# A routed expert layer with 96 places per expert, and its product's bf16 cast on ScalarE

## The chip, the cores and the metric

The kernel runs on one core of a Trainium2 chip. The metric is the device time of one execution in microseconds (us), the median over runs. TensorE is called PE here, VectorE DVE, ScalarE ACT, GpSimd POOL, SyncE SP.

## What is computed

The reference is two blocks of two layers each (two mixers of attention, two hybrid mixers of gated linear attention and a state space scan), each layer with a feed-forward network. The last of the four feed-forward networks is a mixture of eight experts, and the change lies there alone:

```python
def swiglu_2(t, w_gate, w_up, w_down):
    return (jax.nn.silu(t @ w_gate) * (t @ w_up)) @ w_down

def moe_swiglu(h, router_w, w_gate, w_up, w_down):
    ...
    logits = (t @ router_w).astype(jnp.float32)
    top_v, top_i = lax.top_k(logits, TOP_K)
    top_p = jax.nn.softmax(top_v, axis=-1)
    gates = jnp.sum(jax.nn.one_hot(top_i, N_EXPERTS, dtype=jnp.float32) * top_p[..., None], axis=1)
    ...
    for e in range(N_EXPERTS):
        out = out + gates[:, e:e + 1] * swiglu_2(t, w_gate[e], w_up[e], w_down[e])
```

There are 256 tokens of 1024 values, a hidden width of 3584, eight experts and two experts per token. So 512 token copies are spread over the experts, 64 on average. With the reference's inputs the fullest expert gets 92. All weights and activations are float32.

## The kernel before, in words

**Splitting.** A float32 operand is taken as a sum of two bf16 numbers: hi is the value rounded to bf16, lo is the remainder. A product is made of three bf16 matmuls, hi by hi, hi by lo and lo by hi. For every weight, ACT makes hi (a cast) and DVE makes lo (the weight less hi).

**Places.** Router, counts and picks come first. Each expert has 128 places; the tokens that chose it are gathered by matmuls with 0/1 matrices into `he_hi` and `he_lo` (expert, k tile, place). The largest count is put in `COUNT`. If it fits into the places, `gathered` runs (from `moe_parts`, lines 1168 to 1375), else `general`, which sends all 256 tokens through every expert. PE, ACT and DVE each test this for themselves (lines 2388, 2397, 2408).

**Pieces.** An expert's hidden width is cut into 28 pieces of 128, 224 in all. A piece has 128 x 3072 float32 weights: gate and up (2048 columns, the front, 1 MB) and down (1024 columns, the back, 0.5 MB). SP loads them into a ring of four slots, `RING`, front and back by DMAs of their own, in the order front, back of the piece before, front (lines 341 to 350). A front slot comes free with DVE's lo (semaphore `front_used`), a back slot with DVE's lo of down (`back_used`).

**A pair of pieces** is the unit of all engines:

- PE, `up` (lines 1186 to 1197): 2 x 8 x 3 matmuls a piece; the weights stand still (128 x 128) and an expert's places stream (128 columns) into half of a bank of PSUM. PE then does `down` (lines 1199 to 1209) of the pair before: 6 matmuls a piece, the hidden values stand still (128 x 128 places) and 512 columns of down weights stream. So the order is up, up, down, down.
- ACT, `silus`: SiLU of the pair (line 1275, 256 columns for two pieces), then hi of gate/up of piece 4 (1264), hi of down of piece 2 (1270), gate/up 5, down 3 (counted from the pair's group of four).
- DVE, `gating`: `gate_pair` multiplies SiLU by up (1322), waits for its own result, casts it to bf16 (1325), makes its lo (1327); then come the four lo: gate/up 4 (1310), down 2 (1315), gate/up 5, down 3.

```python
dve.tensor_tensor(f, silu[p], hid(2 * i, 1, T), ALU.mult).then_inc(S.prod.sem, 1)
dve.wait_ge(S.prod.sem, m + S.prod.at(3))
dve.wait_ge(S.down_done.sem, 2 * m + S.down_done.at(0))
dve.tensor_copy(hi, f).then_inc(S.act_hi.sem, 1)
```

**Border of two experts.** DVE copies the expert's output out of PSUM (`keep_output`, 1331) after the first pair of the next one, and PE scatters it back to the tokens with 8 float32 products of 256 columns (`scatter`, 1214) before the next `down`. Seven borders lie inside the stage.

In the rows below the names are tiles: `weights` is the ring, `normed_or_mix` and `turned` hold the bf16 gate/up weights of slots 0, 1 and 2, 3, `aux` the bf16 down weights, `projected` the gathered tokens, `probs` the SiLU and the bf16 product, `probs_turned` the float32 product, `ps` is PSUM, `extra` the expert's output. The operation that the profile calls CAST or COPY on DVE is `tensor_copy`.

## Time and profile before

| | before |
|---|---|
| median of 3 runs | 2783.81 us (2783.21 to 2789.51) |
| span of the profiled execution | 2779.1 us (its own device time is not given apart) |
| PE busy | 2581.3 us, 93% of the span |
| PE weight loads | 1969.1 us, 71% |
| DVE busy | 1941.8 us, 70% |
| ACT busy | 1431.9 us, 52% |
| DMA | 674.36 MB, mean 243 GB/s |

The span runs from the first to the last instruction of one execution; the median comes from executions without a profiler and has some us around the span in it. Busy shares are averages over many stages with different limits. Matmuls are pipelined and their ends are modelled, so two matmuls of which each is shown 0.22 us long may start 0.06 us apart: PE's pace is read from starts.

### The profile page before, as it was taken

How to read it: one execution, taken by the hardware profiler on the slowest of the kernel's cores; microseconds unless marked ns; L12 is line 12 of the kernel's file. 1: busy time of each engine (PE TensorE's matmuls, PEld its weight loads, DVE VectorE, ACT ScalarE, POOL GpSimd, SP SyncE). 2: the span in 40 equal slices, each digit the busy share in tenths (PEclk: the TensorE clock that was granted, in tenths of full speed). 3: DMA queues.
4: the chain of work that ended last, by engine and by line, in shares of the span. 5: the costliest groups of instructions: out<-in, count | busy, mean ns of one | idle time of the engine just before them, and what ended most of it. 6: DMA issues, size and time to landing. Idle time of an engine off the chain costs nothing. (4 is left out here: it accounts for less than half of the span.)

```text
span 2779.1 us, 57909 instructions
## 1 busy us (share of the span) xinstructions
PE 2581.3 (93%) x22787; PEld 1969.1 (71%) x22998; DVE 1941.8 (70%) x2633; ACT 1431.9 (52%) x1753; POOL 14.9 (1%) x12
## 2 busy tenths in 40 slices
PE   6988899999887789998899999899999999999997
PEld 4646677676754467767677767678888888888886
DVE  3366555655535755555565555689999999999997
ACT  3245444443312554444354444377777676777774
POOL 0000000000200000000000000000000000000000
PEclk8979999999978999999899998889999999999999
DMA  7331555554366056544465544449999999999994
GB/s 290 143 161 35 216 199 201 209 201 173 109 229 271 1 201 222 194 162 181 164 251 199 192 168 182 152 178 404 386 395 383 375 392 376 392 381 379 393 376 192
DMA packets 121211, 674.36 MB, mean 243 GB/s; under 512 B 13488, under 2 KB 13968, under 8 KB 67088
## 3 DMA queue, kind: packets, MB, share of 16 engines
q1 hardware_dynamic: 120032, 664.47, 63.4%
q10 hardware_dynamic: 1072, 8.42, 0.8%
q8 instruction: 72, 1.18, 0.2%
q14 instruction: 35, 0.29, 0.0%
HBM read 671.79 MB, written 1.05 MB: 242 GB/s over the span
## 5 line engine op out<-in xcount | busy, mean ns | idle before, releaser
L940 PE MATMUL ps<-projected,normed_or_mix 128*128 128x256 bf16 x1504 | 409.9, 273 | 1.2 <-issue 1.2
L941 PE MATMUL ps<-projected,normed_or_mix 128*128 128x256 bf16 x1504 | 409.9, 273 | 0.0
L1194 PE MATMUL ps<-projected,normed_or_mix 128*128 (+1 forms) x1792 | 304.6, 220 | 3.3 <-DVEq L1342 3.3
L1196 PE MATMUL ps<-projected,normed_or_mix 128*128 (+1 forms) x1792 | 304.7, 220 | 0.0
L1195 PE MATMUL ps<-projected,normed_or_mix 128*128 (+1 forms) x1792 | 304.6, 220 | 0.0
L1196 PE MATMUL ps<-projected,turned 128*128 (+1 forms) x1792 | 303.1, 219 | 0.0
L1195 PE MATMUL ps<-projected,turned 128*128 (+1 forms) x1792 | 303.0, 219 | 0.0
L1194 PE MATMUL ps<-projected,turned 128*128 (+1 forms) x1792 | 303.0, 219 | 0.0
L1315 DVE TENSOR_TENSOR aux<-weights,aux 128x1024 bf16<-128x1024 f32 x224 | 273.0, 1219 | 0.4 <-ACT aux L1270 0.2
L1310 DVE TENSOR_TENSOR normed_or_mix<-weights,normed_or_mix 128x2048 bf16<-128x2048 f32 x111 | 253.9, 2287 | 6.9 <-ACT normed_or_mix L1264 6.9
L1310 DVE TENSOR_TENSOR turned<-weights,turned 128x2048 bf16<-128x2048 f32 x112 | 256.2, 2287 | 3.5 <-ACT turned L1264 3.5
L1270 ACT ACTIVATE aux<-weights 128x1024 bf16<-128x1024 f32 x224 | 234.1, 1045 | 19.3 <-PE ps L1208 19.3
L1264 ACT ACTIVATE normed_or_mix<-weights 128x2048 bf16<-128x2048 f32 x111 | 211.1, 1902 | 16.5 <-DMA weights<-moe 13.0
L805 PE MATMUL ps<-weights_halves,normed_or_mix_halves 128*128 128x512 f32 (+4 forms) x576 | 218.8, 380 | 0.0
L1264 ACT ACTIVATE turned<-weights 128x2048 bf16<-128x2048 f32 x112 | 213.0, 1902 | 10.5 <-DMA weights<-moe 9.6
L942 PE MATMUL ps<-projected,normed_or_mix 128*128 128x256 bf16 x752 | 205.0, 273 | 0.0
L942 PE MATMUL ps<-projected,aux 128*128 128x256 bf16 x752 | 205.0, 273 | 0.0
L972 DVE TENSOR_TENSOR probs_turned<-probs,ps 128x256 f32<-128x256 f32 x94 | 39.6, 421 | 229.2 <-ACT probs L965 229.2
L965 ACT ACTIVATE probs<-ps 128x256 f32<-128x256 f32 x94 | 36.0, 383 | 295.4 <-PE ps L942 295.1
L1194 PEld LDWEIGHTS ps<-projected,normed_or_mix 128*128 128x128 bf16 x1792 | 175.9, 98 | 10.2 <-issue 3.7
L1195 PEld LDWEIGHTS ps<-projected,normed_or_mix 128*128 128x128 bf16 x1792 | 175.9, 98 | 6.5
L1194 PEld LDWEIGHTS ps<-projected,turned 128*128 128x128 bf16 x1792 | 175.3, 98 | 6.5
(385 smaller groups left out, 5863.5 us busy)
## 6 DMA issues: line engine op xcount, KB each, us to landing
weights<-moe SPq DMA_DIRECT2D x224, 1024.0 KB, 7.6
weights<-moe SPq DMA_DIRECT2D x224, 512.0 KB, 5.8
weights<-l_ffn SPq DMA_DIRECT2D x66, 1024.0 KB, 5.1
weights<-ada SPq DMA_DIRECT2D x64, 1024.0 KB, 5.6
weights<-l_ffn SPq DMA_DIRECT2D x66, 512.0 KB, 5.5
weights<-ada SPq DMA_DIRECT2D x64, 512.0 KB, 6.1
weights<-ffn SPq DMA_DIRECT2D x28, 1024.0 KB, 5.1
weights<-w_in SPq DMA_DIRECT2D x24, 948.0 KB, 4.7
```

What stands on the lines that cost most here:

```text
L805: pe.matmul(o, h_hi(k)[:, t], lo, start=False, stop=False)
L940: pe.matmul(o, hi, h_hi(k), start=(k == 0), stop=False)
L941: pe.matmul(o, hi, h_lo(k), start=False, stop=False)
L942: mm = pe.matmul(o, lo, h_hi(k), start=False, stop=(k == KD - 1))
L972: dve.tensor_tensor(f, silu[p][:, 0:width], hid[p][:, T:T + width], ALU.mult).then_inc(S.prod.sem, 1)
L1194: pe.matmul(o, hi[:, t], xh, start=(k == 0), stop=False)
L1195: pe.matmul(o, hi[:, t], xl, start=False, stop=False)
L1196: mm = pe.matmul(o, lo[:, t], xh, start=False, stop=(k == KD - 1))
L1264: act.activation(gu4[j % SLOTS][0], RING[:, slot(j), 0:2 * D], ACT.Copy).then_inc(S.hi_gu.sem, 1)
L1270: act.activation(down4[j % SLOTS][0], RING[:, slot(j), 2 * D:3 * D], ACT.Copy).then_inc(S.hi_d.sem, 1)
L1310: dve.tensor_tensor(gu4[j % SLOTS][1], RING[:, slot(j), 0:2 * D], gu4[j % SLOTS][0], ALU.subtract).then_inc(front_used.sem, 1)
L1315: dve.tensor_tensor(down4[j % SLOTS][1], RING[:, slot(j), 2 * D:3 * D], down4[j % SLOTS][0], ALU.subtract).then_inc(back_used.sem, 1)
```

## The change

- `CAP = 96` takes the place of 128 wherever places are counted: the streamed columns of `up` (128 to 96), the standing columns of `down` (128 to 96), the output rows that are kept and scattered (128 to 96), SiLU, product, cast and remainder of a pair (256 to 192 columns), and the test of `COUNT`. The gathering before the stage still makes 128 places.
- The bf16 cast of the product leaves DVE. ACT does it as `product_hi`, behind the cast of the next gate/up piece and ahead of the casts of down 2, gate/up 5 and down 3. It waits for DVE's multiply (`S.prod`) and for old `down` products.
- DVE, after the multiply, takes the lo of gate/up 4 (`between`), then waits for ACT's cast (`S.act_hi`) and makes the product's lo; the rest of its order is unchanged.

```diff
--- before.py
+++ after.py
@@ -41,6 +41,8 @@
 GQ, GK, GV, GG, GA, SZ, SDT, L2N, CONV = 0, 256, 512, 1024, 1536, 1552, 2064, 2072, 768
 
 F0, F2, NE = 2816, 3584, 8
+
+CAP = 96
 
 
 ROWS = {
@@ -1179,8 +1181,8 @@
         gate_col = lambda k: ADA[:, 3, 5 * KD + k, 2:3]
         gated = lambda k: (HT[:, k // 2, k % 2 * T:(k % 2 + 1) * T], PS[:, k // 2, k % 2 * T:(k % 2 + 1) * T])
 
-        def hid(c, w, width=PB, at=0):
-            return PS[:, 6 + c // 2 % 2, w * T + at:w * T + at + width]
+        def hid(c, w, width=CAP, at=0):
+            return PS[:, 6 + c // 2 % 2, w * 2 * CAP + at:w * 2 * CAP + at + width]
 
         def products(pe):
             def up(e, j, c, m):
@@ -1189,8 +1191,8 @@
                 hi, lo = gu4[j % SLOTS]
                 for w in range(2):
                     for k in range(KD):
-                        o, t = hid(j, w, PB, j % 2 * PB), slice(w * D + k * PB, w * D + (k + 1) * PB)
-                        xh, xl = (v[:, bass.ds(e * D + k * PB, PB)] for v in (he_hi, he_lo))
+                        o, t = hid(j, w, CAP, j % 2 * CAP), slice(w * D + k * PB, w * D + (k + 1) * PB)
+                        xh, xl = (v[:, bass.ds(e * D + k * PB, CAP)] for v in (he_hi, he_lo))
                         pe.matmul(o, hi[:, t], xh, start=(k == 0), stop=False)
                         pe.matmul(o, hi[:, t], xl, start=False, stop=False)
                         mm = pe.matmul(o, lo[:, t], xh, start=False, stop=(k == KD - 1))
@@ -1199,20 +1201,20 @@
             def down(j, c, m, start=False, stop=False):
                 pe.wait_ge(back_used.sem, c + (a + 1))
                 pe.wait_ge(S.act_done.sem, m + S.act_done.at(3))
-                hi, lo = (hid_hl[j // 2 % 2][h][:, j % 2 * PB:(j % 2 + 1) * PB] for h in range(2))
+                hi, lo = (hid_hl[j // 2 % 2][h][:, j % 2 * CAP:(j % 2 + 1) * CAP] for h in range(2))
                 w_hi, w_lo = down4[j % SLOTS]
                 for h, bank in enumerate((4, 5)):
-                    t = slice(h * 512, (h + 1) * 512)
-                    pe.matmul(PS[:, bank, :], hi, w_hi[:, t], start=start, stop=False)
-                    pe.matmul(PS[:, bank, :], hi, w_lo[:, t], start=False, stop=False)
-                    mm = pe.matmul(PS[:, bank, :], lo, w_hi[:, t], start=False, stop=stop)
+                    t, o = slice(h * 512, (h + 1) * 512), PS[0:CAP, bank, :]
+                    pe.matmul(o, hi, w_hi[:, t], start=start, stop=False)
+                    pe.matmul(o, hi, w_lo[:, t], start=False, stop=False)
+                    mm = pe.matmul(o, lo, w_hi[:, t], start=False, stop=stop)
                 mm.then_inc(S.down_done.sem, 1)
 
             def scatter(e):
                 pe.wait_ge(expert_kept.sem, e + 1)
                 for k in range(KD):
-                    pe.matmul(PS[:, k // 2, k % 2 * T:(k % 2 + 1) * T], oe[:, k * PB:(k + 1) * PB],
-                              put_t[:, bass.ds(e, 1), :].rearrange("p o t -> p (o t)"), start=False, stop=False,
+                    pe.matmul(PS[:, k // 2, k % 2 * T:(k % 2 + 1) * T], oe[0:CAP, k * PB:(k + 1) * PB],
+                              put_t[0:CAP, bass.ds(e, 1), :].rearrange("p o t -> p (o t)"), start=False, stop=False,
                               skip_group_check=True)
 
             def four(e, g, first=False, ahead=True, begins=False, ends=False):
@@ -1272,7 +1274,13 @@
             def silu_pair(i, m):
                 act.wait_ge(S.up_done.sem, 2 * m + S.up_done.at(4))
                 act.wait_ge(S.prod.sem, m + S.prod.at(1))
-                act.activation(silu[i % 2], hid(2 * i, 0, T), ACT.Silu).then_inc(S.silu_done.sem, 1)
+                act.activation(silu[i % 2][:, 0:2 * CAP], hid(2 * i, 0, 2 * CAP), ACT.Silu).then_inc(S.silu_done.sem, 1)
+
+            def product_hi(i, m):
+                act.wait_ge(S.prod.sem, m + S.prod.at(3))
+                act.wait_ge(S.down_done.sem, 2 * m + S.down_done.at(0))
+                act.activation(hid_hl[i % 2][0][:, 0:2 * CAP], hid_f[i % 2][:, 0:2 * CAP],
+                               ACT.Copy).then_inc(S.act_hi.sem, 1)
 
             gate_up(1, 1, False)
             down(0, 0, False)
@@ -1284,16 +1292,21 @@
                 silu_pair(i, i)
                 for j in (2 * i + 2, 2 * i + 3):
                     gate_up(j + 2, j + 2)
+                    if j % 2 == 0:
+                        product_hi(i, i)
                     down(j, j, j >= SLOTS)
             with act.Fori(1, n // SLOTS - 1) as g:
                 for i in range(2):
                     silu_pair(i, 2 * g + i)
                     for j in (2 * i + 2, 2 * i + 3):
                         gate_up(j + 2, g * SLOTS + (j + 2))
+                        if j % 2 == 0:
+                            product_hi(i, 2 * g + i)
                         down(j, g * SLOTS + j)
             for i in range(2):
                 m = n // 2 - 2 + i
                 silu_pair(i, m)
+                product_hi(i, m)
                 for j in (2 * i + 2, 2 * i + 3):
                     if i == 0:
                         down(j, n - SLOTS + j)
@@ -1315,29 +1328,27 @@
                 dve.tensor_tensor(down4[j % SLOTS][1], RING[:, slot(j), 2 * D:3 * D], down4[j % SLOTS][0],
                                   ALU.subtract).then_inc(back_used.sem, 1)
 
-            def gate_pair(i, m):
+            def gate_pair(i, m, between=lambda: None):
                 p = i % 2
-                f, hi, lo = hid_f[p], hid_hl[p][0], hid_hl[p][1]
+                f, hi, lo, s = (v[:, 0:2 * CAP] for v in (hid_f[p], hid_hl[p][0], hid_hl[p][1], silu[p]))
                 dve.wait_ge(S.silu_done.sem, m + S.silu_done.at(1))
-                dve.tensor_tensor(f, silu[p], hid(2 * i, 1, T), ALU.mult).then_inc(S.prod.sem, 1)
-                dve.wait_ge(S.prod.sem, m + S.prod.at(3))
-                dve.wait_ge(S.down_done.sem, 2 * m + S.down_done.at(0))
-                dve.tensor_copy(hi, f).then_inc(S.act_hi.sem, 1)
+                dve.tensor_tensor(f, s, hid(2 * i, 1, 2 * CAP), ALU.mult).then_inc(S.prod.sem, 1)
+                between()
                 dve.wait_ge(S.act_hi.sem, m + S.act_hi.at(1))
                 dve.tensor_tensor(lo, f, hi, ALU.subtract).then_inc(S.act_done.sem, 1)
 
             def keep_output(e):
                 dve.wait_ge(S.down_done.sem, e * fc + S.down_done.at(fc + 2))
-                dve.tensor_copy(oe, PS[:, 4:6, :].rearrange("p a n -> p (a n)")).then_inc(expert_kept.sem, 1)
+                dve.tensor_copy(oe[0:CAP, :], PS[0:CAP, 4:6, :].rearrange("p a n -> p (a n)")).then_inc(expert_kept.sem, 1)
 
             def four(c, m, kept=None):
                 for i in range(2):
-                    gate_pair(i, m + i)
+                    gate_pair(i, m + i, lambda: gate_up(2 * i + 4, c + (2 * i + 4)))
                     if i == 0 and kept is not None:
                         keep_output(kept)
-                    for j in (2 * i + 2, 2 * i + 3):
-                        gate_up(j + 2, c + (j + 2))
-                        down(j, c + j)
+                    down(2 * i + 2, c + (2 * i + 2))
+                    gate_up(2 * i + 5, c + (2 * i + 5))
+                    down(2 * i + 3, c + (2 * i + 3))
 
             dve.sem_inc(S.act_done.sem, 2)
             dve.sem_inc(S.prod.sem, 2)
@@ -2385,7 +2396,7 @@
 
             @block.tensor
             def _(pe):
-                few = pe.value_load(COUNT[0:1, 0:1], min_val=0, max_val=T) <= PB
+                few = pe.value_load(COUNT[0:1, 0:1], min_val=0, max_val=T) <= CAP
                 with pe.If(few):
                     gathered[0](pe)
                 with pe.Else():
@@ -2394,7 +2405,7 @@
 
             @block.scalar
             def _(act):
-                few = act.value_load(COUNT[0:1, 0:1], min_val=0, max_val=T) <= PB
+                few = act.value_load(COUNT[0:1, 0:1], min_val=0, max_val=T) <= CAP
                 steps = act_step.n
                 with act.If(few):
                     gathered[1](act)
@@ -2405,7 +2416,7 @@
 
             @block.vector
             def _(dve):
-                few = dve.value_load(COUNT[0:1, 0:1], min_val=0, max_val=T) <= PB
+                few = dve.value_load(COUNT[0:1, 0:1], min_val=0, max_val=T) <= CAP
                 steps = dve_step.n
                 with dve.If(few):
                     gathered[2](dve)
```

The order of DVE in one pair of the inner loop, before (`turned`: gate/up weights, `aux`: down weights):

```order
L1322 TENSOR_TENSOR probs_turned<-probs,ps 128x256 [waits silu_done]
L1324 ISA [waits product_made]
L1325 CAST probs<-probs_turned 128x256 [waits down_done]
L1327 TENSOR_TENSOR probs<-probs_turned,probs 128x256 [waits hidden_hi]
L1310 TENSOR_TENSOR turned<-weights,turned 128x2048 [waits hi_gate_up]
L1315 TENSOR_TENSOR aux<-weights,aux 128x1024 [waits hi_down]
L1310 TENSOR_TENSOR turned<-weights,turned 128x2048 [waits hi_gate_up]
L1315 TENSOR_TENSOR aux<-weights,aux 128x1024 [waits hi_down]
```

and with the change:

```order
L1335 TENSOR_TENSOR probs_turned<-probs,ps 128x192 [waits silu_done]
L1323 TENSOR_TENSOR turned<-weights,turned 128x2048 [waits hi_gate_up]
L1338 TENSOR_TENSOR probs<-probs_turned,probs 128x192 [waits hidden_hi]
L1328 TENSOR_TENSOR aux<-weights,aux 128x1024 [waits hi_down]
L1323 TENSOR_TENSOR turned<-weights,turned 128x2048 [waits hi_gate_up]
L1328 TENSOR_TENSOR aux<-weights,aux 128x1024 [waits hi_down]
```

The cast at line 1325 is gone, the first of the four lo stands between the multiply and the product's lo, and the product has 192 columns.

The order of ACT in one pair of the inner loop, before:

```order
L1275 ACTIVATE probs<-ps 128x256 [waits product_made]
L1264 ACTIVATE turned<-weights 128x2048 [waits up_done]
L1270 ACTIVATE aux<-weights 128x1024 [waits down_done,slot_back_in3]
L1264 ACTIVATE turned<-weights 128x2048 [waits up_done]
L1270 ACTIVATE aux<-weights 128x1024 [waits down_done,slot_back_in0]
```

and with the change:

```order
L1277 ACTIVATE probs<-ps 128x192 [waits product_made]
L1266 ACTIVATE turned<-weights 128x2048 [waits up_done]
L1281 REGISTER_ALU [waits product_made]
L1282 ACTIVATE probs<-probs_turned 128x192 [waits down_done]
L1272 ACTIVATE aux<-weights 128x1024 [waits down_done,slot_back_in3]
L1266 ACTIVATE turned<-weights 128x2048 [waits up_done]
L1272 ACTIVATE aux<-weights 128x1024 [waits down_done,slot_back_in0]
```

Between the first and the second weight cast stands the new cast of the product (line 1282), and it waits for DVE's multiply (`product_made`, at line 1281) before the other three casts of the pair can start.

## Rows read from the trace of the kernel before

**Rows 1.** The page, part 2: 40 slices of 69.5 us, DMA share and rate

```profile
DMA  7331555554366056544465544449999999999994
GB/s 290 143 161 35 216 199 201 209 201 173 109 229 271 1 201 222 194 162 181 164 251 199 192 168 182 152 178 404 386 395 383 375 392 376 392 381 379 393 376 192
```

**Rows 2.** Stretches: length, busy us of each engine, PEclk, DMA share, GB/s

```profile
10.00:47.00 37.00, 25.73 (x166) 14.86 (x168) 12.71 (x29) 12.39 (x27) 0.00 (x0) 0.77 1.02 416
...
2130.00:2146.00 16.00, 15.89 (x220) 13.17 (x220) 15.65 (x15) 11.75 (x10) 0.00 (x0) 1.00 1.01 415
2200.00:2300.00 100.00, 99.36 (x1355) 82.42 (x1366) 96.08 (x87) 74.25 (x63) 0.00 (x0) 1.00 0.99 384
```

**Rows 3.** DVE in order of time: start us, length us, engine, line; two multiplies

```profile
1857.96 0.41 DVE L1322 TENSOR_TENSOR probs_turned<-probs,ps 128x256 f32<-128x256 f32 x1
...
2746.34 0.41 DVE L1322 TENSOR_TENSOR probs_turned<-probs,ps 128x256 f32<-128x256 f32 x1
```

**Rows 4.** ACT in order of time, idle us before in brackets

```profile
2222.56 0.38 ACT L1275 ACTIVATE probs<-ps 128x256 f32<-128x256 f32 x1 [2.08 <-PE ps L1196]
2222.84 1.90 ACT L1264 ACTIVATE normed_or_mix<-weights 128x2048 bf16<-128x2048 f32 x1
2224.64 1.05 ACT L1270 ACTIVATE aux<-weights 128x1024 bf16<-128x1024 f32 x1
2225.59 1.90 ACT L1264 ACTIVATE normed_or_mix<-weights 128x2048 bf16<-128x2048 f32 x1
...
2230.51 0.38 ACT L1275 ACTIVATE probs<-ps 128x256 f32<-128x256 f32 x1 [2.08 <-PE ps L1196]
```

**Rows 5.** DVE and PE around the second border: multiplies and the scatter

```profile
2073.39 0.41 DVE L1322 TENSOR_TENSOR probs_turned<-probs,ps 128x256 f32<-128x256 f32 x1
...
2080.11 3.67 PE L1214 MATMUL ps<-extra 128*128 x16
...
2100.75 0.41 DVE L1322 TENSOR_TENSOR probs_turned<-probs,ps 128x256 f32<-128x256 f32 x1
```

**Rows 6.** PE in order of time: first and last of 11 wide, of 9 narrow

```profile
2198.65 0.38 PE L1207 MATMUL ps<-aux,probs 128*128 128x512 bf16 x1
...
2200.80 0.38 PE L1208 MATMUL ps<-aux,probs 128*128 128x512 bf16 x1
...
2201.80 0.22 PE L1196 MATMUL ps<-projected,normed_or_mix 128*128 x1
...
2202.25 0.22 PE L1195 MATMUL ps<-projected,normed_or_mix 128*128 x1
```

**Rows 7.** DVE in order of time, one pair while DVE sets the pace

```profile
1881.67 0.41 DVE L1322 TENSOR_TENSOR probs_turned<-probs,ps 128x256 f32<-128x256 f32 x1
...
1882.89 2.29 DVE L1310 TENSOR_TENSOR normed_or_mix<-weights,normed_or_mix 128x2048 bf16<-128x2048 f32 x1
1885.09 1.22 DVE L1315 TENSOR_TENSOR aux<-weights,aux 128x1024 bf16<-128x1024 f32 x1
...
1889.57 0.41 DVE L1322 TENSOR_TENSOR probs_turned<-probs,ps 128x256 f32<-128x256 f32 x1
1890.13 0.29 DVE L1325 CAST probs<-probs_turned 128x256 bf16<-128x256 f32 x1
1890.45 0.42 DVE L1327 TENSOR_TENSOR probs<-probs_turned,probs 128x256 bf16<-128x256 f32 x1
```

**Rows 8.** DMA issues: tensors, queue, count, KB each, median us to landing

```profile
weights<-moe SPq DMA_DIRECT2D x224, 1024.0 KB, 7.6
...
weights<-ffn SPq DMA_DIRECT2D x28, 1024.0 KB, 5.1
```

**Rows 9.** PE's weight loads (PEld) in order of time, two merged

```profile
315.49 0.13 PEld L1007 LDWEIGHTS ps<-zeros_bf 128*128 128x128 bf16 x2 [1.61 <-issue]
```

**Rows 10.** ACT early in the stage, waits for loads

```profile
1880.21 1.91 ACT L1264 ACTIVATE normed_or_mix<-weights 128x2048 bf16<-128x2048 f32 x1 [2.45 <-DMA weights<-moe]
...
1884.00 1.91 ACT L1264 ACTIVATE normed_or_mix<-weights 128x2048 bf16<-128x2048 f32 x1 [0.93 <-DMA weights<-moe]
```

## The prediction

> **What bounds the kernel now.** I read the slices of the page first. From about 1850 us to the end of the routed experts every engine and the DMA engines are busy together: DMA is at nine tenths or more, at 375 to 395 GB/s [rows 1]. So the stage of 224 weight pieces decides, and the change touches nothing else. The stretches confirm it: of 100 us in the middle PE is busy 99.36, DVE 96.08, ACT 74.25, DMA 0.99, at the full clock (1.00, the level of 2.4 GHz) [rows 2].
>
> Work comes in pairs of pieces, and the multiplies (DVE, line 1322) mark them, one for each two of the 224. From the one at 1857.96 us to the one at 2746.34 us are 109 pairs, 888.4 us, 8.15 us each [rows 3]. Inside an expert a pair takes 7.95 us, SiLU to SiLU (2222.56 to 2230.51) [rows 4]. Across the border from one expert to the next, the three pairs from 2073.39 to 2100.75 take 27.36 us instead of 23.85: a border costs 3.5 us, and there are seven [rows 5]. 109 x 7.95 + 7 x 3.5 = 891, close to the 888.
>
> Three things want nearly the same 7.95 us.
>
> *PE.* Matmuls of 512 columns start 0.215 us apart (ten steps in 2.15 us), those of 128 columns 0.056 apart (eight steps in 0.45 us, 0.0555 taken) [rows 6]. A pair has 96 of the narrow and 12 of the wide: 5.33 + 2.58 = 7.91 us. The border's scatter is 3.67 us of float32 matmuls [rows 5], and it shows almost in full in the 3.5 us. ACT sits idle 2.08 us until PE's products are there [rows 4]. So PE sets the pace, by a hair.
>
> *DVE.* Where DVE set the pace itself, early in the stage, a pair took 7.90 us (1881.67 to 1889.57) with no idle time in it [rows 7].
>
> *DMA.* A pair is 2 x 1.573 MB = 3.146 MB, at 7.95 us 396 GB/s. The queue is hardly ever empty: a load of 1 MB lands 7.6 us after its issue here, 5.1 us in the dense layer, where it finds the queue free [rows 8]. About 2.5 us of transfers stand ahead of each load.
>
> **The change part by part.**
>
> *96 columns in place of 128 (gate and up matmuls).* Between 128 columns (0.0555 us) and 512 (0.215) a column costs 0.000415 us, so 96 columns cost 0.0555 - 32 x 0.000415 = 0.0422 us. 96 of them: 4.05 us, with the unchanged 12 wide ones (their weights are now 96 columns, what streams is still 512) 6.63 us. PE gives back 1.28 us a pair. This needs weight loads that can follow each other every 0.042 us. Two loads of 128 columns, each shown 0.10 long, take 0.13 together, so they start 0.03 apart [rows 9]. I take the full gain. The scatter contracts over 96 rows in place of 128 but streams the same columns: unchanged, 3.67 us.
>
> The Trainium skill says otherwise of weight loads: TensorE: Matmul & The Clock Gate, section LDWEIGHTS (loading the stationary operand), gives columns / 1.2 ns, which is 107 ns for 128 columns. By that rule narrower moving tiles would win nothing; the rows, already at 55 ns with a new weight load for every matmul, do not agree with it.
>
> *Narrower elementwise work.* A DVE row of 2048 takes 2.29 us, of 1024 1.22 [rows 7]: 0.00104 us a column, so 64 columns fewer save 0.067 us, in the multiply and in the subtraction: 0.13.
>
> *The cast moves from DVE to ACT.* It goes from DVE with 0.32 us (1890.13 to 1890.45) [rows 7]. The multiply also loses the wait for its own result: the next start came 0.56 after it although it lasts 0.41, and where no operation waits for the one before, the next starts some 0.08 before the end (2.29 long, next at 2.20). So 0.56 becomes 0.41 - 0.08 = 0.33: another 0.23. DVE pair: 7.90 - 0.13 - 0.32 - 0.23 = 7.22 us. ACT gets the cast: a row of 2048 takes 1.90 and one of 1024 1.05 [rows 4], 0.00083 a column, so 192 columns are 0.35 long, 0.25 from start to start. ACT pair: 0.28 + 2 x (1.80 + 0.95) + 0.25 = 6.0 us. There is room.
>
> *The new wait.* ACT now stops at the cast until DVE has multiplied, and behind it on ACT's queue stand the casts of down piece 2, gate/up piece 5 and down piece 3 of the group, and the next SiLU. The first gate/up cast stands before it, and DVE has this piece's remainder (2.2 us) to do meanwhile. The longest closed way is: multiply 0.33, six ACT operations 6.0, then DVE's four remainders and the subtraction of that turn 6.95 (1882.89 to 1889.57 is 6.68 [rows 7], and 0.27), for two pairs: 13.3 us, 6.65 a pair. Cover is there as long as this stays under what sets the pace. DVE's subtraction is 2.2 us later than before, but PE's down product of that pair comes only after two up products; with PE at 6.63 in a longer pair nothing is late by it. SP's order of loads is unchanged: the slots come free in the same order.
>
> *What is left: DMA.* Compute now allows 7.22 us a pair, 436 GB/s. No row reaches that. The bounds: 385 GB/s is what the stage averages now with 0.99 busy; 416 GB/s ran from 10 to 47 us with the queue full, and 415 in one stretch of this stage [rows 2]. A full queue must carry at least today's 396 inside an expert, and the standing backlog of 2.5 us says it is not far above. I take 397, nearest to the stage's own pace, and not 416, since other stretches of the same stage fall under 390 at the same share. Pair: 3.146 / 0.397 = 7.92 us. What is gained is then mostly the borders: a border's 3.5 us on PE is hidden, as PE has 1.3 us to spare in each pair and DMA goes on loading.
>
> **The sum.** 109 x 7.92 = 863.3 us in place of 888.4: -25.1. At the end the last two up products of the stage lie open: 96 x 0.0133 = -1.3. Together -26 us. The profiled span is 2779.1, so 2753 after; the median of the runs is 2783.8, 4.7 above the span, so **2758 us** (the time of the profiled execution itself is not shown apart from its span, and I carry the difference over).
>
> **The rivals.** About 0.3% (8.4 us) is what a measurement of this kernel can tell from no change.
>
> *A, forecast (0.71):* DMA is the bound at 389 to 408 GB/s: 8.09 to 7.71 us a pair, 2776 to 2734.
>
> *B (0.10): the DMA engines run clean* at 408 to 416: 7.71 to 7.56 a pair, 2734 to 2718. For it: 415 in one stretch here. Against: the mean of 385 with a busy share of 0.99.
>
> *C (0.04): PE does not get faster,* since weight loads set 0.0555. Then 7.95 and the borders stay: 2784, the same. Against it: loads 0.03 apart [rows 9].
>
> *D (0.08): DMA is at its limit already,* under 389: 109 x 8.1 = 883, 2777 to 2784, the same. For it: the backlog and ACT's waits for loads, 2.45 us once [rows 10]. Against: 396 is carried inside every expert.
>
> By the DMA page of the Trainium skill (DMA: Bandwidth & Descriptors, Specifications) a core gets about 358 GB/s from HBM. Then a pair could not take under 8.79 us; the stage's 385 is already above it, so the page does not hold for this core running alone.
>
> *E (0.05), slower: the new wait closes a loop with late loads.* Place: ACT's casts behind the hidden cast. ACT used to run ahead of DVE and took a late load on its own; now it may not pass DVE's multiply, so its waits for loads add to the 13.3 us of the way above. It decides once they exceed 3.0 us in two pairs (2 x 8.15 - 13.3). The early stretch shows 2.45 and 0.93 for successive loads of one pair [rows 10]: if every two pairs carried 3.4 us, 8.35 a pair, 109 x 0.20 = +22, 2805. Against: a load's landing would have to slip by more than the slot's own slack, and late loads mean a DMA-bound pace, which is case A.
>
> *F (0.02), the change doesn't take the short path:* an expert with more than 96 tokens sends all through the general code with 256 columns, at least 224 x 3.9 = +870 us. The routing of the reference's inputs gives the fullest expert 92 tokens, so it should not.
>
> **How the numbers follow.** Faster = A + B = 0.81, same = C + D = 0.12, slower = E + F = 0.07. The range takes in A whole (0.71), the slower half of B (0.05, down to 2726) and the half of D next to A (0.04, up to 2780), and leaves out the rest, 0.20: 2726 to 2780.
>
> **What would show it.** In the profile after: up matmuls 0.042 apart; DVE with idle time of 0.3 to 0.9 us a pair, ended by ACT casts that themselves waited for loads of the experts' weights; DMA 0.99 or more at 393 to 405 GB/s; 1 MB loads landing after 9 us or more in place of 7.6; no pair of 9.4 at a border; multiplies 7.8 to 8.0 apart. PE busy by records stays high, since their ends are modelled. It is wrong if ACT's idle time before the hidden cast is followed by idle DVE without a load behind it (E), if up matmuls stay 0.055 apart (C), or if DVE runs without gaps at 7.2 to 7.5 (B).

## The result, and the profile after

The changed kernel takes **2716.74 us** (median of 4 runs, 2713.40 to 2718.32), the kernel before, beside it, 2783.51 (2780.92 to 2789.51): a ratio of 0.9755, with a 95% interval of 0.974 to 0.977. Forecast were 2758 us and a range of 2726 to 2780. The direction was right. The gain is 67 us where 26 were forecast, and it lies outside the range, 9 us past its fast end.

The 40 slices of the page of the changed kernel, 67.8 us each, DMA share and rate:

```profile
DMA  7340555554466127545275545338999999999995
GB/s 297 120 191 24 212 203 206 210 200 156 148 227 243 62 99 257 196 177 208 110 260 198 208 157 206 111 138 335 417 414 401 418 418 418 418 408 418 418 416 228
```

The full slices of the routed stage now run at 401 to 418 GB/s, where they had 375 to 404 [rows 1]. What stands ahead of it moves about as before.

Stretches of the changed kernel (length, busy us of each engine, PEclk, DMA share, GB/s):

```profile
2200.00:2300.00 100.00, 93.36 (x1456) 76.75 (x1453) 98.08 (x82) 83.22 (x80) 0.00 (x0) 1.00 1.02 418
1860.00:2660.00 800.00, 746.88 (x11504) 611.26 (x11502) 780.18 (x639) 658.95 (x633) 0.00 (x0) 1.00 1.02 414
```

Against [rows 2], PE has fallen from 99.36 to 93.36 of 100 and ACT has risen from 74.25 to 83.22. DMA went from a share of 0.99 at 384 GB/s to 1.02 at 418, the level of [rows 2]'s 10 to 47 us and of its stretch at 2130.

DVE of the changed kernel in order of time (start, length), the same two multiplies as in [rows 3]:

```profile
1855.81 0.35 DVE L1335 TENSOR_TENSOR probs_turned<-probs,ps 128x192 f32<-128x192 f32 x1
...
2682.76 0.35 DVE L1335 TENSOR_TENSOR probs_turned<-probs,ps 128x192 f32<-128x192 f32 x1
```

109 pairs now take 826.95 us, 7.59 each, where they took 888.4 (8.15): 61.4 of the 68.0 us by which the span shrank (2779.1 to 2711.1). The first of these multiplies stands 2.2 us earlier already, no more than two executions of the kernel before differ by (executed again it has this multiply at 1855.36 us), and what follows the last one is 4.4 us shorter.

ACT of the changed kernel, one pair inside an expert, SiLU to SiLU, with the idle time before in brackets:

```profile
2240.35 0.31 ACT L1277 ACTIVATE probs<-ps 128x192 f32<-128x192 f32 x1
2241.36 1.91 ACT L1266 ACTIVATE normed_or_mix<-weights 128x2048 bf16<-128x2048 f32 x1 [0.70 <-DMA weights<-moe]
2243.33 0.36 ACT L1282 ACTIVATE probs<-probs_turned 128x192 bf16<-128x192 f32 x1
2243.60 1.04 ACT L1272 ACTIVATE aux<-weights 128x1024 bf16<-128x1024 f32 x1
2245.13 1.91 ACT L1266 ACTIVATE normed_or_mix<-weights 128x2048 bf16<-128x2048 f32 x1 [0.49 <-DMA weights<-moe]
...
2247.89 0.31 ACT L1277 ACTIVATE probs<-ps 128x192 f32<-128x192 f32 x1
```

The pair takes 7.54 us, and 3.146 MB in 7.53 us is 418 GB/s. In [rows 4] ACT stood 2.08 us at each SiLU until PE was done. That wait is gone here, and in its place ACT waits for the loads of both gate/up pieces.

DVE of the changed kernel, one pair right after a border, where the loads have run ahead:

```profile
2086.23 0.34 DVE L1335 TENSOR_TENSOR probs_turned<-probs,ps 128x192 f32<-128x192 f32 x1
2086.50 2.28 DVE L1323 TENSOR_TENSOR turned<-weights,turned 128x2048 bf16<-128x2048 f32 x1
2088.70 0.35 DVE L1338 TENSOR_TENSOR probs<-probs_turned,probs 128x192 bf16<-128x192 f32 x1
...
2092.31 1.22 DVE L1328 TENSOR_TENSOR aux<-weights,aux 128x1024 bf16<-128x1024 f32 x1
2093.44 0.35 DVE L1335 TENSOR_TENSOR probs_turned<-probs,ps 128x192 f32<-128x192 f32 x1
```

Without idle time a pair takes 7.21 us, where [rows 7] had 7.90. The multiply is followed by the next operation after 0.27 us, no longer after 0.56.

PE of the changed kernel, two up products with 47 between them:

```profile
2206.00 0.21 PE L1196 MATMUL ps<-projected,normed_or_mix 128*128 x1
...
2208.04 0.21 PE L1196 MATMUL ps<-projected,normed_or_mix 128*128 x1
```

48 steps in 2.04 us are 0.0425 apart, where [rows 6] had 0.0555. Each of these matmuls has a weight load of its own, shown 0.10 us long. The Trainium skill (TensorE: Matmul & The Clock Gate, LDWEIGHTS (loading the stationary operand)) puts a load at columns / 1.2 ns, by which 128 columns take an estimated 107 ns. The trace agrees with that for the length of one load, but it is no floor for the step from one to the next.

DMA issues of the changed kernel (count, KB each, median us to landing), against 7.6 in [rows 8]:

```profile
weights<-moe SPq DMA_DIRECT2D x224, 1024.0 KB, 8.5
weights<-moe SPq DMA_DIRECT2D x224, 512.0 KB, 6.6
```

### The profile page after: what moved, and what is told of

It reads as the page before. It is cut to its first block and busy times, and to the rows that moved or that the text cites. A ratio compares the mean times of both kernels' runs of the same rounds, so it can differ in the third digit from the quotient of the medians.

```text
span 2711.1 us, 58120 instructions
## 1 busy us (share of the span) xinstructions
PE 2462.7 (91%) x22998; PEld 1860.1 (69%) x22998; DVE 1890.3 (70%) x2521; ACT 1471.5 (54%) x1865; POOL 14.9 (1%) x12
## 5 line engine op out<-in xcount | busy, mean ns | idle before, releaser
L1196 PE MATMUL ps<-projected,normed_or_mix 128*128 (+1 forms) x1792 | 234.6, 207 | 3.3 <-DVEq L1353 3.3
L1198 PE MATMUL ps<-projected,normed_or_mix 128*128 (+1 forms) x1792 | 234.6, 207 | 0.0
L1197 PE MATMUL ps<-projected,normed_or_mix 128*128 (+1 forms) x1792 | 234.6, 207 | 0.0
L1196 PE MATMUL ps<-projected,turned 128*128 (+1 forms) x1792 | 233.0, 206 | 0.7 <-DVE turned L1323 0.7
L1198 PE MATMUL ps<-projected,turned 128*128 (+1 forms) x1792 | 233.0, 206 | 0.0
L1197 PE MATMUL ps<-projected,turned 128*128 (+1 forms) x1792 | 233.0, 206 | 0.0
L1208 PE MATMUL ps<-aux,probs 128*96 128x512 bf16 x448 | 172.6, 385 | 45.9 <-DVE probs L1338 45.9
```

Source lines behind the costliest of these rows:

```text
L1196: pe.matmul(o, hi[:, t], xh, start=(k == 0), stop=False)
L1197: pe.matmul(o, hi[:, t], xl, start=False, stop=False)
L1198: mm = pe.matmul(o, lo[:, t], xh, start=False, stop=(k == KD - 1))
L1208: pe.matmul(o, hi, w_hi[:, t], start=start, stop=False)
```

## The experiments

Two questions were open. Where does the gain of 41 us more than forecast come from? And is the kernel now really bound by its loads? Eleven kernels ran, in three groups, each beside the kernel before (its median was 2783.01, 2782.92 and 2783.25 us in the three). In what follows, the steady pair is the median step between DVE's multiplies over the whole stage, and the rows give 1860 to 2600 us of each kernel (length, busy us of PE, PEld, DVE, ACT and POOL, PEclk, DMA share, GB/s). The changed kernel has in that view:

```profile
1860.00:2600.00 740.00, 689.59 (x10595) 564.39 (x10593) 721.61 (x592) 609.26 (x586) 0.00 (x0) 1.00 1.01 414
```

### The 96 places alone

```diff
@@ ACT: silus @@
-                    if j % 2 == 0:
-                        product_hi(i, 2 * g + i)
@@ DVE: gate_pair, four @@
-                between()
+                dve.wait_ge(S.prod.sem, m + S.prod.at(3))
+                dve.wait_ge(S.down_done.sem, 2 * m + S.down_done.at(0))
+                dve.tensor_copy(hi, f).then_inc(S.act_hi.sem, 1)
```

> 96 places, but the bf16 cast of the product stays on DVE, in its old place between multiply and subtraction. Theory A (the pair takes the longest of PE 6.63, DMA 7.53, DVE): DVE is 7.90 less 3 x 0.06 for the narrower product = 7.73 us a pair, so it is the bound, 109 x (8.15 - 7.73) = 46 less some 7 x 1.2 for the output copy at each border: about 2745 us, and DVE without gaps. Rival B (the loads of the experts' weights could not go faster than 396 GB/s beside the old arrangement, and the moved cast freed them): the pair stays at 7.9 us or more and the time at 2765 or above, with ACT waiting for loads.

Measured: 2742.77 us (2738.75 to 2746.56), a ratio of 0.986 (0.9838 to 0.9881), -40 us. The steady pair is 7.74 us, by DVE (stretch, then DVE in order of time):

```profile
1860.00:2600.00 740.00, 688.51 (x10343) 554.26 (x10340) 723.00 (x671) 561.98 (x474) 0.00 (x0) 1.00 1.00 402
```

```profile
2204.88 0.35 DVE L1330 TENSOR_TENSOR probs_turned<-probs,ps 128x192 f32<-128x192 f32 x1
2205.38 0.26 DVE L1333 CAST probs<-probs_turned 128x192 bf16<-128x192 f32 x1
2205.67 0.36 DVE L1335 TENSOR_TENSOR probs<-probs_turned,probs 128x192 bf16<-128x192 f32 x1
...
2212.62 0.35 DVE L1330 TENSOR_TENSOR probs_turned<-probs,ps 128x192 f32<-128x192 f32 x1
```

This alone refutes the 397 GB/s of the prediction's main term (not yet its range, which went up to 408). The loads now run at 3.146 / 7.74 = 406 GB/s inside an expert, where the forecast held 397 to be what they could do, and all this run did was to let the engines ask for more.

Its waits for loads hold a warning (engine, line, waited for: us, times, longest):

```profile
ACT normed_or_mix L1266 <- DMA weights<-moe: 81.9, 86, 3.5
ACT turned L1266 <- DMA weights<-moe: 79.1, 90, 3.0
```

ACT waits 161 of 740 us for loads here. The changed kernel's two lines, over the same 740 us, add up to 85:

```profile
ACT turned L1266 <- DMA weights<-moe: 44.2, 73, 2.0
ACT normed_or_mix L1266 <- DMA weights<-moe: 40.7, 70, 1.3
```

Still DVE has no gap in this run's pair. ACT has room, it runs ahead of DVE, and a load can't start before DVE has given its slot back. Such waits do not tell which of the two is the bound.

### The moved cast alone

```diff
-CAP = 96
+CAP = 128
```

> 128 places, with the cast on ACT and DVE taking the next remainders between. Theory A: PE still needs 7.91 us a pair and 3.5 us at each border, DVE would need 7.35; so PE is the bound and nothing is gained: 2780 to 2784 us, pairs 7.95 us, DVE with some 0.6 us idle a pair. Rival B: if DVE or the loads set the old pace, the pair falls to 7.5 and the time to about 2735.

Measured: 2783.57 us (2779.29 to 2786.61), a ratio of 1.0001 (0.9991 to 1.0011): nothing.

```profile
1860.00:2600.00 740.00, 740.00 (x9863) 608.83 (x9861) 681.21 (x551) 560.83 (x544) 0.00 (x0) 1.00 0.99 385
```

PE is busy through all 740 us, the steady pair is 7.95 again, and DVE's time went down from the 96.08 of 100 in [rows 2] to 92 without any use. The parts do not add: -40 and 0 alone, -67 together. Narrower matmuls move the bound from PE (7.95) to DVE (7.74), the moved cast takes DVE to 7.21, and the loads' 7.53 stands in between.

### 96 places, with PE as slow as before

Three more matmuls of 512 columns in each down product, to put PE back to 6.63 + 6 x 0.215 = 7.92 us a pair. They add repeated products to the sum.

```diff
                     pe.matmul(o, hi, w_lo[:, t], start=False, stop=False)
+                    for _ in range(2 - h):
+                        pe.matmul(o, hi, w_hi[:, t], start=False, stop=False)
```

> The changed kernel with three more matmuls of 512 columns a piece in the down product (6 to 9; the output has hi x hi several times in place of once). PE 4.05 + 18 x 0.2155 = 7.93 us a pair. Theory A: 7.95 us a pair, about 2780 us. It also asks what slowed the loads before: if a pace that leaves the DMA queue short of work gives the low rates (as low as 355 to 385 GB/s in stretches, with the DMA engines shown busy 0.97 to 1.0), they come back here, and 1 MB loads land after 7 to 8 us; if the 128 columns or the chip of that moment did it, the rate here is an even 396 GB/s and loads land after 6 to 7 us.

Measured in a single execution: 2787.78 us, steady pair 7.97.

```profile
1860.00:2600.00 740.00, 740.00 (x10387) 583.99 (x10384) 668.11 (x549) 552.33 (x544) 0.00 (x0) 1.00 0.99 384
```

With all of the change in place and only PE slow, the stage is back at 384 GB/s with a share of 0.99, the very figures of [rows 2]. Its 1 MB loads land after 7.6 us, as in [rows 8]. So both signs that the forecast took for a limit of the loads come from PE's pace.

### The kernel before, once more

No edit.

> The kernel before, unchanged, profiled once more on this chip. If the uneven loads belong to this kernel, stretches of 16 us spread from 355 to 415 GB/s again and 1 MB loads land after 7.6 us in the median. If they belonged to the moment of the first profile, the rates are even and loads land after about 6 us. The time is 2784 us either way, since PE sets the pace.

Measured in a single execution: 2778.39 us, steady pair 7.95.

```profile
1860.00:2600.00 740.00, 740.00 (x9853) 608.40 (x9851) 713.26 (x643) 534.67 (x453) 0.00 (x0) 1.00 0.99 386
```

386 GB/s again in a second execution, beside kernels that ran at 402: the low rate is not a matter of the moment. The unevenness is there again too. Cut into stretches of 16 us, the stage runs at 343 to 413 GB/s here and ran at 345 to 420 in the first execution, with the steady pair at 7.95 us in both. The 1 MB loads land after 7.7 us.

### The changed kernel with half of the front loads

```diff
-        w = min(PART, src.shape[1])
+        w = min(PART, src.shape[1]) // part
...
-                        load_front(sp, item(g * SLOTS + (i + lag + j)), n + lag + j)
+                        load_front(sp, item(g * SLOTS + (i + lag + j)), n + lag + j, 2 if name == "moe" else 1)
```

In the stage's loops the up weights are not loaded; the instructions of PE, DVE and ACT stay as they are.

> The changed kernel, with the front loads of the expert stage's loops half as long: the gate weights (1024 columns, 0.52 MB a piece) are loaded, the up weights are not, so that the products use whatever those columns of the buffers held. A pair of pieces then needs 2.1 MB in place of 3.15 MB; the instructions of TensorE, VectorE and ScalarE stay as they are. Theory A (loads are the bound of the changed kernel, with VectorE's 7.21 us per pair just below their 7.53): the pair falls to VectorE's pace of 7.21 to 7.25 us, ScalarE's waits for loads vanish, the DMA engines fall to a share of about 0.75, and 109 pairs are 786 to 790 us in place of 827: about 2680 us, ratio 0.987 (2675 to 2690). Theory B (the 7.53 us is a chain between VectorE, ScalarE and TensorE, and the loads only follow it): the pair stays at 7.5, 2715 us. Theory C (loads slow the compute engines themselves, by sharing memory): single instructions of VectorE get shorter than 2289 and 1224 ns and the pair comes below 7.1 us, under 2670 us.

Measured: 2695.35 us (2690.10 to 2698.43), ratio 0.9685 (0.9669 to 0.9701), 21 us under the changed kernel.

```profile
1860.00:2600.00 740.00, 709.60 (x10918) 580.93 (x10917) 730.89 (x608) 609.74 (x603) 0.00 (x0) 1.00 0.83 284
```

This is theory A. The steady pair falls from 7.53 to 7.21 us, DVE's pace as it was seen after a border. The loads did bound the changed kernel. B is out, and so is C: the gate/up remainder is 2282 ns here in place of 2289.

The run came out 15 us slower than the 2680 expected, because the estimate left out the borders. DVE, PE and ACT around one of them:

```profile
2052.56 0.35 DVE L1335 TENSOR_TENSOR probs_turned<-probs,ps 128x192 f32<-128x192 f32 x1
...
2055.29 1.22 DVE L1342 COPY extra<-ps 96x1024 f32<-96x1024 f32 x1
2056.68 3.71 PE L1216 MATMUL ps<-extra 96*128 x16 [1.58 <-DVE extra L1342]
2060.90 0.35 DVE L1335 TENSOR_TENSOR probs_turned<-probs,ps 128x192 f32<-128x192 f32 x1
...
2067.18 0.33 ACT L1277 ACTIVATE probs<-ps 128x192 f32<-128x192 f32 x1 [1.59 <-PE ps L1198]
2069.34 2.29 DVE L1323 TENSOR_TENSOR normed_or_mix<-weights,normed_or_mix 128x2048 bf16<-128x2048 f32 x1 [0.89 <-ACT normed_or_mix L1266]
```

This pair takes 8.34 us, 1.13 over, by DVE's copy of the expert's output. The next but one takes 8.19 (2068.10 to 2076.29), and that comes from PE: its scatter waits for the copy and takes 3.71 us, so ACT gets the later up products 1.59 us late, and DVE waits 0.89 us for the cast behind them. That is 2.1 us a border. At two of the seven borders the scatter takes 5.40 us in place of 3.71, at a granted clock that has fallen (0.64 from 2160 to 2164 us, after PE had waited 1.58 us), and the pair between the two long ones takes 8.80 in place of 7.21. Together some 18 us. The changed kernel has the same long pairs at its borders (8.5 and 8.2, twice 8.8), but the loads go on meanwhile, and up to four pairs of 7.21 us behind them, in place of 7.53, make most of it good.

### The kernel before with half of the front loads

The same edit in the kernel before.

> The same halved front loads in the kernel before (the up weights of the expert stage's loops are not loaded). Theory A (TensorE's 7.95 us per pair bounds the kernel before, and what the uneven loads cost it lies only in the difference of 8.15 to 7.95 per pair): the steady pair stays at 7.9 to 7.95, and the time falls by at most 109 x 0.2 = 22 us if the gaps at borders and after late loads were loads' doing, to 2762 to 2783 us. Theory B (the kernel before is bound by loads too, at its own lower rate): the pair falls below 7.9 and the time by over 25 us.

Measured: 2782.17 us (2777.56 to 2788.89), ratio 0.9996 (0.9986 to 1.0006).

```profile
1860.00:2600.00 740.00, 735.18 (x9764) 608.49 (x9852) 713.49 (x640) 531.20 (x454) 0.00 (x0) 1.00 0.75 257
```

A third fewer bytes in each pair and not a microsecond less: steady pair 7.95, the pairs of a border still 9.38 and 9.50. So the loads did not bound the kernel before. PE did, borders and all, and DVE in the first expert [rows 7]. The DMA engines' 0.99 had cost nothing, and there was headroom behind it.

### 112 places

```diff
-CAP = 96
+CAP = 112
```

> The changed kernel with 112 places in place of 96. Theory A (loads bound at 7.53 us per pair): TensorE's pair is 96 x 0.049 + 2.58 = 7.28 us by the mean of the up products at 96 and 128 columns, VectorE's is about 7.27, both below 7.53, so the pair stays at the loads' pace and only the borders' catching up is slower: 2718 to 2726 us, ratio to the changed kernel 1.001 to 1.004. Theory B (the places set the pace through TensorE and VectorE): halfway between the kernels with 128 and 96 places, 2750 us.

Measured: 2721.18 us (2716.86 to 2723.15), ratio 0.9776 (0.9760 to 0.9792), 4 us above the changed kernel. The intervals overlap, so these 4 us are not clear of noise.

```profile
1860.00:2600.00 740.00, 736.64 (x10584) 627.40 (x10584) 726.85 (x591) 615.47 (x584) 0.00 (x0) 1.00 1.01 413
```

PE goes from 689.59 to 736.64 us, the steady pair stays at 7.52, the rate at 413 GB/s. Between 128 and 112 places lie 62 us, between 112 and 96 lie 4. The gain does not scale with the columns; it ends where the loads take over.

### The cast on ScalarE, without the remainder in between

```diff
                 dve.tensor_tensor(f, s, hid(2 * i, 1, 2 * CAP), ALU.mult).then_inc(S.prod.sem, 1)
-                between()
                 dve.wait_ge(S.act_hi.sem, m + S.act_hi.at(1))
                 dve.tensor_tensor(lo, f, hi, ALU.subtract).then_inc(S.act_done.sem, 1)
+                between()
```

> The changed kernel with the cast left on ScalarE, but VectorE waits for it and subtracts before it takes the next gate and up remainder (the place in which the kernel before had its own cast). Theory A: VectorE's pair is 7.21 us plus its wait for the cast, which takes ScalarE some 0.27 us and two signals of 0.1 to 0.2 us, and longer when ScalarE is inside its next cast of weights: 7.75 to 8.2 us per pair, 24 to 75 us more than the changed kernel: 2740 to 2790 us, likeliest 2755. Theory B (the remainder in between does not matter, since loads are the bound and VectorE has room): 2717 us.

Measured: 2762.13 us (2760.41 to 2765.17), ratio 0.9925 (0.9908 to 0.9941), 45 us above the changed kernel. Its steady pair is 7.81, and DVE in order of time shows why:

```profile
2209.16 0.34 DVE L1335 TENSOR_TENSOR probs_turned<-probs,ps 128x192 f32<-128x192 f32 x1
2210.01 0.36 DVE L1337 TENSOR_TENSOR probs<-probs_turned,probs 128x192 bf16<-128x192 f32 x1 [0.51 <-ACT probs L1282]
...
2216.96 0.34 DVE L1335 TENSOR_TENSOR probs_turned<-probs,ps 128x192 f32<-128x192 f32 x1
```

The subtraction starts 0.85 us after the multiply, not 0.27: 0.58 more a pair, 7.21 + 0.58 = 7.79. On ACT the cast stands ready for a whole microsecond before its input is there:

```profile
2209.61 0.36 ACT L1282 ACTIVATE probs<-probs_turned 128x192 bf16<-128x192 f32 x1 [1.02 <-DVE probs_turned L1335]
```

So it is not that ACT is busy. The way over to ACT and back is what costs. It explains the steady pair, 0.28 us over 7.53 or some 31 us in all; the other 15 or so lie at the borders. There PE waits 3.4 to 3.6 us for DVE's copy, the granted clock falls from its higher level (1.00, 2.4 GHz) to its lower (0.50, 1.2 GHz), and the scatter takes 5.40 to 6.44 us at all seven borders, where the first run, with waits of at most 1.21 us, has 3.72. One of these scatters, and the stretch that it lies in:

```profile
2299.71 6.41 PE L1216 MATMUL ps<-extra 96*128 x16 [3.49 <-DVE extra L1342]
```

```profile
2300.00:2304.00 4.00, 4.00 (x10) 3.20 (x10) 4.00 (x4) 1.69 (x1) 0.00 (x0) 0.50 0.97 373
```

With the cast left on DVE (the first run) the kernel takes 2742.77, with the cast moved but waited for on the spot 2762.13, with the remainder put in between 2716.74. Moving the cast is worth something only because of what was put in the gap.

### The changed kernel with less work on DVE

```diff
-                    pe.matmul(o, hi, w_lo[:, t], start=False, stop=False)
+                    pe.matmul(o, hi, (w_hi if h else w_lo)[:, t], start=False, stop=False)
...
-                dve.tensor_tensor(down4[j % SLOTS][1], RING[:, slot(j), 2 * D:3 * D], down4[j % SLOTS][0],
-                                  ALU.subtract).then_inc(back_used.sem, 1)
+                dve.tensor_tensor(down4[j % SLOTS][1][:, 0:512], RING[:, slot(j), 2 * D:2 * D + 512],
+                                  down4[j % SLOTS][0][:, 0:512], ALU.subtract).then_inc(back_used.sem, 1)
```

> The changed kernel with VectorE's down remainder taken over 512 of its 1024 columns; for the other half TensorE multiplies by the high part again in place of the remainder, so its work stays. That leaves out half of the down weights' low parts. VectorE's pair falls from 7.21 to about 6.1 us; TensorE's is 6.63, ScalarE's about 6.0. Theory A (loads are the bound at 7.53): the steady pair stays at 7.5 us, the stretches of 7.21 us after borders go faster only until the loads have been caught up, and the time falls by no more than what a stage of 7.565 a pair has above 7.5: 111 x 0.06 = 7 us, 2709 to 2716 us. Theory B (VectorE's work or its place in the chain still sets the pair): 7.565 falls towards 6.7 and the time by over 50 us.

Measured: 2715.11 us (2710.69 to 2717.25), ratio 0.9751 (0.9733 to 0.9769). The changed kernel in the same group: 2717.87.

```profile
1860.00:2600.00 740.00, 695.84 (x10698) 570.39 (x10696) 626.09 (x596) 604.96 (x588) 0.00 (x0) 0.99 1.02 416
```

```profile
2222.28 0.69 DVE L1328 TENSOR_TENSOR aux<-weights,aux 128x512 bf16<-128x512 f32 x1
2223.56 2.29 DVE L1323 TENSOR_TENSOR turned<-weights,turned 128x2048 bf16<-128x2048 f32 x1 [0.60 <-ACT turned L1266]
```

DVE lost 95 us of work in this stretch and the kernel won 3 us at most. The steady pair is 7.53, and DVE's spare time shows as waits of 0.60 us for casts that themselves wait for loads. The rate stays where it was, at 416 GB/s.

### Both: half of the front loads, less work on DVE

> Both at once: the front loads of the expert stage's loops half as long (the up weights not loaded) and VectorE's down remainder over half of its columns. Loads then need a share of about 0.9, VectorE 6.1, ScalarE 6.0 us a pair. Theory A: the next bound is TensorE's 6.63 to 6.7 us per pair, against 7.21 in the run with halved loads alone: 109 x 0.5 to 0.6 = 55 to 65 us below that run's 2695, 2632 to 2645 us. Theory B (a chain between the engines of about 7.2 us that no single engine's busy time shows): the pair stays above 7.1, about 2690 us.

Measured: 2644.66 us (2640.76 to 2645.60), ratio 0.9491 (0.9472 to 0.9509), 51 us under the run with half of the loads alone.

```profile
1860.00:2600.00 740.00, 740.00 (x11673) 614.12 (x11672) 674.69 (x649) 650.15 (x641) 0.00 (x0) 1.00 0.87 304
```

PE is busy for all 740 us and the steady pair is 6.67. This is the 6.63 of the prediction, which no other run could show because loads or DVE always stood above it. The pairs alone would give 111 x 0.54 = 60 us; the borders take back some 10, since PE now pays for its scatter there (the mean over the stage is 6.91, 0.24 above the steady pair, against 0.15 with DVE as the bound).

### The changed kernel, once more

No edit.

> The changed kernel once more, beside the other runs of this call: 2717 us (2713 to 2721), the stage's loads at 414 to 418 GB/s with a share of 1.02, the steady pair 7.53 us. If its loads fell to 385 to 400 GB/s in this execution, the rate would be a matter of the moment and not of the kernel's pace, and it would need 2740 to 2770 us.

Measured: 2717.87 us (2715.66 to 2718.81), ratio 0.9759 (0.9742 to 0.9777), steady pair 7.52.

```profile
1860.00:2600.00 740.00, 688.93 (x10603) 563.78 (x10600) 722.07 (x593) 610.16 (x585) 0.00 (x0) 1.00 1.02 414
```

The rate of 414 GB/s belongs to the kernel, as the 385 belonged to the other.

All of them side by side, by what sets the steady pair:

| kernel | bound | steady pair, us | DMA share | GB/s | median, us |
|---|---|---|---|---|---|
| before | PE | 7.95 | 0.99 | 386 | 2783.5 |
| before, half of the front loads | PE | 7.95 | 0.75 | 257 | 2782.2 |
| moved cast alone | PE | 7.95 | 0.99 | 385 | 2783.6 |
| change, PE slowed | PE | 7.97 | 0.99 | 384 | 2787.8 |
| change, no remainder between | DVE | 7.81 | 1.00 | 393 | 2762.1 |
| 96 places alone | DVE | 7.74 | 1.00 | 402 | 2742.8 |
| change, 112 places | loads | 7.52 | 1.01 | 413 | 2721.2 |
| **the change** | loads | 7.53 | 1.01 | 414 | 2716.7 |
| change, less DVE work | loads | 7.53 | 1.02 | 416 | 2715.1 |
| change, half of the front loads | DVE | 7.21 | 0.83 | 284 | 2695.4 |
| change, both | PE | 6.67 | 0.87 | 304 | 2644.7 |

(Shares and rates are means over 1860 to 2600 us.)

## Why the prediction came out as it did

**PE sets the pace before: right, and more so than argued.** The forecast said "by a hair", with DVE at 7.90 and the loads at 396 GB/s as close seconds. DVE was that close. The loads were not: a third of the bytes taken away changed nothing.

**Up matmuls 0.0422 apart: right.** 0.0425 in the trace, and a pair of 6.67 against 6.63 once nothing else was in the way.

**DVE's pair 7.22: right.** 7.21, and the parts as well: 7.74 with the cast still on DVE, where the forecast's parts give 7.90 - 0.13 = 7.77.

**ACT has room and the new wait costs nothing: right.** ACT idles over 1 us a pair, and before the hidden cast mostly without a wait. Rival E's loop did not close. What the wait would have cost uncovered is now known, 45 us (with what it does to PE's clock at the borders), and the cover that the forecast named (the 2.2 us remainder) is what hides it.

**Borders hidden: right.** 109 pairs at 7.53 would be 820.8 us, and they took 826.95. Of 7 x 3.5 = 24.5 us at borders 6 are left. The forecast had PE's 1.3 us to spare in mind; it named neither DVE's copy of 1.2 us nor a fall of PE's clock behind a wait, and these too are mostly hidden, since DVE's 7.21 lies 0.32 under the loads' 7.53.

**The loads' rate: wrong, and this is the step that failed.** The prediction put it so: "I take 397, nearest to the stage's own pace, and not 416". Measured are 418 GB/s inside an expert and 414 over the stage. With 416 the forecast's own sum gives 109 x (3.146 / 0.416) = 824.3 us, 64.1 less than 888.4, 1.3 more at the end, so 2718 us; 2716.74 were measured. So 40 of the 41 us come from this one term. (In detail the 109 pairs took 2.7 us more than these 824.3, and the start and the end of the stage, of which the sum counted 1.3, gave 6.6, of which 2.2 can't be put down to the change.)

Three readings carried it, and each fell:

- *"A full queue must carry at least today's 396 ... and the standing backlog of 2.5 us says it is not far above."* The 396 was not what the queue could carry; it was what PE asked for, 3.146 MB each 7.95 us. The kernel with PE slowed shows the same rate and the same 7.6 us to landing. The landing time goes with how early the loads are issued: it grew to 8.5 us when the kernel became faster, and to 9.1 with less work on DVE at the same pace. It was read against the dense layer's 5.1 us as a sign of saturation, without a row of a queue that was known to be full.
- *"Other stretches of the same stage fall under 390 at the same share."* The share is not the fraction of a capacity in use. From 2200 to 2300 us it reads 0.99 at 384 GB/s [rows 2], where PE loses no time to a load and 9% more is still to be had (418 in the changed kernel). In stretches of 16 us of the kernel before, the same share of 1.01 to 1.02 goes with 366, 380 and 417 GB/s, and the 96 places alone show 1.01 at 405 GB/s from 2200 to 2300 us, with DVE as the bound:

```profile
2100.00:2116.00 16.00, 15.89 (x216) 13.12 (x217) 15.65 (x15) 11.85 (x12) 0.00 (x0) 1.00 1.01 366
2164.00:2180.00 16.00, 15.89 (x216) 13.16 (x217) 15.65 (x15) 11.85 (x11) 0.00 (x0) 1.00 1.01 380
2244.00:2260.00 16.00, 15.89 (x220) 13.17 (x219) 15.65 (x16) 11.84 (x11) 0.00 (x0) 1.00 1.02 417
```

- *The 415 and 416 of [rows 2] were set aside as the exception.* The 415 ran in a stretch in which PE set the pace (the multiplies from 2124.60 to 2148.45 us stand 7.95 apart), and so did the 417 above. No stretch can be faster than the DMA engines are, so the fastest ones say what they can do at least; the slower ones only say what was asked of them. The fast ones should have been the estimate and the slower ones the doubt. The forecast's "375 to 395" also leaves out the first slice of the stage, at 404 [rows 1]. Rival B had the right mechanism, and the measured time lies just past its fast end (2718 to 2734); it got 0.10. Rival D (0.08) rested on the same misreading.

Of the signs that the forecast named, DVE's idle time came as forecast (7.53 less 7.21 is 0.32 us a pair, where 0.3 to 0.9 were named), and no pair takes 9.4 us at a border (the longest take 8.8). The rate (414 to 418, not 393 to 405), the landing time (8.5 us, not 9 or more) and the step of the multiplies (7.53, not 7.8 to 8.0) did not.

A page would have helped here: the Trainium skill (HBM Reference, Specifications (TRN2)) gives about 358 GB/s as a core's share when both cores of a pair stream, and about 425 for a core that streams alone. The prediction weighed only the 358, and rightly threw it out. The 414 to 418 of these runs are close to the other figure. By 425 an estimate of the pair is 7.40 us, still above DVE's 7.22, and the bound the same.

What stays open is how the slower rate comes about at a share of 0.99, that is, what the DMA engines do in the time in which they show as busy and move 385 and not 418. That it goes with the pace of PE is shown (PE slowed, and the kernel before repeated). That the queue then runs short of work at times is the likely reason, but only argued: no row shows it.

No version beyond the changed kernel is in sight from these runs without fewer bytes: 827 us for 109 pairs stand 6 us above the 821 that the loads alone would take, and with 13% less work on DVE at most 3 of them were got back.

## What to carry to other kernels

The rate at which a stage loads is the pace of whatever bounds it, so it says nothing of what the DMA engines can do; and neither a share of 0.99 nor one of 1.01 does. Take the capacity from the fastest stretches (here 415 to 420 GB/s), and test the bound by loading less: if halving the larger loads leaves the time as it is, they were no limit.

Before an engine is relieved, list the pair time of every other one: 7.95 (PE), 7.90 (DVE), 7.53 (loads), 6.0 (ACT). A change that lowers only the highest gains the step to the next, and one that lowers only the second gains nothing, while both together gain more than their sum.

When a small step is handed to another engine, put independent work between handing it over and needing it back. The same cast on ScalarE cost 19 us against leaving it on VectorE when it was waited for at once (some 8 of them in the steady pairs, the rest at the borders), and won 26 us with one remainder in between.

## What was unexpected of the hardware

- The DMA engines' busy share and their rate part ways. With loads of 1 MB and 0.5 MB, a share of 0.99 carried 384 GB/s (388 for a full share) and 1.02 carried 418 (410). The kernels with half of the front loads carry less for a unit of share (0.75 with 257, so 343), but nearly all of their packets are under 8 KB, where in the kernel before 56% are, and no run here tells the two apart. 1 MB loads in the changed kernel take longer to land (8.5 us against 7.6) while more bytes arrive.
- A single round from DVE to ACT and back, for a cast of 0.36 us on an idle ACT, takes 0.85 us from the start of the multiply to that of the subtraction. With the cast on DVE itself it is 0.79 (2204.88 to 2205.67, in the run with 96 places alone). The crossing costs a little more than the handing over saves.
- Weight loads of 128 columns can follow each other every 42.5 ns, each ahead of a matmul of 96 columns, at a granted clock of 1.00.
- A wait of PE can cost a second time after it has ended. Where PE had waited 3.4 to 3.6 us (the run without the remainder in between), the granted clock fell at every border, in places down to 0.50, and a scatter of 3.72 us took 5.40 to 6.44. Behind two waits of 1.90 us in the changed kernel it fell once and once not (scatters of 5.40 us at 2382.67 and of 3.72 us at 2277.27). What decides between the two is not shown.
